# A hybrid delta-rule and attention layer on one core: the delta-rule query left unscaled, its squares joined to the output's norm, and new places for the steps of the mix stage

## What is computed

```python
def l2_normalize(x):
    return x * lax.rsqrt(jnp.sum(jnp.square(x), axis=-1, keepdims=True) + NORM_EPS)

q, k, v = jnp.split(silu(causal_depthwise_conv(qkv, conv_w)), ...)
q = l2_normalize(q); k = l2_normalize(k)
q = q * DK ** -0.5
...
o = einsum('bhck,bhkv->bhcv', q_dec, S) + einsum('bhcs,bhsv->bhcv', qk_intra, v_new)
S = S * g_last + einsum('bhck,bhcv->bhkv', k_dec, v_new)
...
o = rms_norm(o, norm_g) * silu(z)
```

## Time and profile before

| what | value |
|---|---|
| median of 3 runs (lowest to highest) | 2838.77 us (2835.92 to 2839.39) |
| the profiled execution, its own time | 2837.48 us |
| its span | 2835.7 us |
| PE busy, instructions | 2778.3 us (98%), 18295 |
| DVE busy | 2033.2 us (72%) |
| ACT busy | 1424.2 us (50%) |
| mix stage with its heads' ends | about 37 to 960 us |

### The profile page before, as it was taken

One profiled execution on the slowest core, in us unless ns is written; L12 is line 12 of the kernel. 1 busy time (PEld: TensorE's weight loads), 2 busy tenths in 40 slices (PEclk: granted clock), 3 DMA queues, 4 the chain that ended last, 5 costly groups with the idle time before them and its releaser, 6 DMA issues.

```text
span 2835.7 us, 51997 instructions
## 1 busy us (share of the span) xinstructions
PE 2778.3 (98%) x18295; PEld 2515.4 (89%) x18295; DVE 2033.2 (72%) x3714; ACT 1424.2 (50%) x2476; POOL 294.7 (10%) x261
## 2 busy tenths in 40 slices
PE   7999999999999999999999999999999999999998
PEld 7999999999999888888888888888888998888886
DVE  6777778777877656667775665656777677788876
ACT  5655665565556434444443443444545555455552
POOL 0000000000000000003630000000280001500024
PEclk9999999999999999999999999999999999999999
DMA  5444344434444455556555555555555444544444
GB/s 197 147 137 146 131 152 133 149 128 151 133 149 135 151 192 182 189 186 214 180 187 191 182 193 179 187 192 182 194 177 181 163 157 159 184 163 148 143 157 169
DMA packets 129664, 472.81 MB, mean 167 GB/s; under 512 B 15072, under 2 KB 15072, under 8 KB 129376
## 3 DMA queue, kind: packets, MB, share of 16 engines
q1 hardware_dynamic: 125568, 457.37, 49.1%
q0 software_dynamic: 3936, 13.34, 1.5%
HBM read 468.39 MB, written 2.25 MB: 166 GB/s over the span
## 4 chain that ended last, share of the span: by engine, by line
PE 88%; DVE 5%; issue 2%; ACT 2%; POOL 2%; DMA 1%; DVEq 0%; POOLq 0%; ACTq 0%
PE bank L305 35%; PE bank L306 18%; PE bank L307 9%; PE bank L308 8%; PE bank L309 8%; DVE mix_solve_m L1914 2%; PE bank L778 1%; DVE w_lo L281 1%; POOL late_sum L454 1%; POOL late_sq L450 1%; ACT w_hi L275 1%; PE bank L823 1%; PE bank L1034 1%; PE bank L1194 0%; ACT mix_f_p L1393 0%
## 5 line engine op out<-in xcount | busy, mean ns | idle before, releaser
L281 DVE TENSOR_TENSOR w_lo<-raw,w_hi 128x1024 fp32r<-128x1024 f32 x862 | 1058.7, 1253 | 160.5 <-ACT w_hi L275 158.0
L275 ACT ACTIVATE w_hi<-raw 128x1024 fp32r<-128x1024 f32 x862 | 897.0, 1054 | 452.5 <-PE bank L306 433.2
L305 PE MATMUL bank<-u,w_hi 128*128 128x512 f32 x2256 | 806.7, 399 | 0.0
L307 PE MATMUL bank<-u,w_hi 128*128 128x272 f32 (+2 forms) x2064 | 640.1, 310 | 9.1 <-DVE w_lo L281 7.5
L305 PE MATMUL bank<-ya,w_hi 128*128 128x512 f32 x1792 | 635.5, 399 | 2.8 <-DVE w_lo L281 2.8
L306 PE MATMUL bank<-u,w_lo 128*128 128x256 f32 x2256 | 634.8, 281 | 0.0
L309 PE MATMUL bank<-u,w_lo 128*128 128x272 f32 (+2 forms) x2064 | 590.0, 286 | 0.0
L308 PE MATMUL bank<-u,w_hi 128*128 128x272 f32 (+2 forms) x2064 | 589.7, 286 | 0.0
L305 PEld LDWEIGHTS bank<-u,w_hi 128*128 128x128 f32 x2256 | 424.3, 188 | 96.4 <-issue 2.8
L306 PE MATMUL bank<-ya,w_lo 128*128 128x256 f32 x1792 | 503.2, 281 | 0.0
L306 PEld LDWEIGHTS bank<-u,w_lo 128*128 128x128 f32 x2256 | 426.1, 189 | 0.5
(11 more groups left out here) (389 smaller groups left out, 3210.3 us busy)
## 6 DMA issues: line engine op xcount, KB each, us to landing
raw<-in_stream SPq DMA_DIRECT2D x864, 512.0 KB, 3.4
mix_row<-rows POOLq DMA_DIRECT2D x16, 408.0 KB, 4.4
xT<-in_xT SPq DMA_DIRECT2D x4, 544.0 KB, 5.5
mix_coef_m<-meta_rows POOLq DMA_DIRECT2D x16, 128.0 KB, 3.4
h<-in_xT POOLq DMA_DIRECT2D x1, 2048.0 KB, 10.0
out_dram<-h SPq DMA_DIRECT2D x4, 512.0 KB, 2.6
consts<-in_consts POOLq DMA_DIRECT2D x1, 1817.0 KB, 9.2
meta_rows<-mix_b_mat POOLq DMA_DIRECT2D x16, 1.0 KB, 2.5
```

Of the source, the lines that this page charges most:

```text
L275: act.activation(w_hi[:, slot], raw[:, slot], ACT.Copy).then_inc(hi_ready, 1)
L281: dve.tensor_tensor(w_lo[:, slot], raw[:, slot], w_hi[:, slot].bitcast(F32), ALU.subtract).then_inc(lo_ready, 1)
L305: pe.matmul(o, a, x, start=first, stop=False)
L307: pe.matmul(o, a, x[:, 0], start=first, stop=False)
```

## The change

- q of gdn is not normalised. The sum, root and scaling of gdn q are gone (one matmul on PE, two activations on ACT, one instruction on DVE per head), and `norm_of_head` counts four lengths.
- `q square` stays, with another scale, but writes into `fq` (free once the fox logits are done) and stands at 129. `o square` writes `sq` as before; a new DVE step, `o add` at 176, adds the two, and the o sum takes that. The o root uses a new constant column, `eps_o`.
- `qk` on PE and `q dec` on DVE wait for k's scaling or q's silu in place of q's scaling. The copy of the next head's fq waits for `o add`; the conv of the next q waits for `q square`.
- `meta` is in three parts of 2, 7 and 6 instructions.
- Many places in the three lists are new (below).
- In the later MLA stage two semaphores are merged into one, with the counts adjusted.

The diff, without the MLA stage's counts and the renamed arguments of `root`:

```diff
@@ constants
     add("eps", np.full((P, 1), EPS, np.float32))
+    add("eps_o", np.full((P, 1), EPS * P * 4 * EPS, np.float32))
@@ places of the mix steps
-            return n * 5 - 4 + ("gdn k", "gdn q", "fox q", "fox k", "gdn o").index(name)
+            return n * 4 - 3 + ("gdn k", "fox q", "fox k", "gdn o").index(name)
         PE_PLAN = (
-            (28, "columns"), (76, "k sum"), (81, "turn"), (87, "kk"), (94, "q sum"), (98, "transpose"), (100, "qk"),
-            (105, "prod", 1), (106, "fq sum"), (109, "step", 1), (110, "fk sum"), (111, "prod", 2), (118, "logits"),
-            (120, "step", 2), (120, "turn v"), (121, "prod", 3), (123, "step", 3), (123, "turn p"), (124, "prod", 4),
-            (126, "step", 4), (128, "fox out"), (128, "prod", 5), (132, "step", 5), (134, "meta v"), (135, "prod", 6),
-            (139, "meta state"), (141, "step", 6), (143, "k state", 0), (147, "v new", 0), (152, "state", 0),
-            (167, "k state", 1), (169, "v new", 1), (171, "state", 1), (179, "o sum"))
+            (28, "columns"), (76, "k sum"), (81, "turn"), (87, "kk"), (89, "qk"), (96, "fq sum"), (98, "transpose"),
+            (103, "prod", 1), (104, "fk sum"), (107, "step", 1), (110, "prod", 2), (113, "step", 2),
+            (115, "logits"), (116, "prod", 3), (119, "step", 3), (120, "turn v"), (124, "prod", 4), (124, "turn p"),
+            (125, "step", 4), (128, "prod", 5), (128, "fox out"), (131, "step", 5), (134, "prod", 6), (140, "meta v"), (142, "meta state"), (142, "step", 6), (143, "k state", 0), (148, "v new", 0), (152, "state", 0),
+            (167, "k state", 1), (169, "v new", 1), (171, "state", 1), (181, "o sum"))
         ACT_PLAN = (
-            (69, "k square"), (69, "k root"), (78, "cols"), (80, "decay"), (82, "q square"), (87, "turned"),
-            (93, "q root"), (101, "fq square"), (105, "fq root"), (105, "fk square"), (111, "fk root"), (114, "soft"),
-            (126, "f v"), (127, "f pt"), (127, "f out"), (137, "v new m"), (141, "state"), (152, "v new", 0),
-            (169, "v new", 1), (175, "o square"), (179, "o root"), (182, "y hi"))
+            (69, "k square"), (69, "k root"), (78, "cols"), (81, "decay"), (87, "turned"),
+            (90, "fq square"), (97, "fq root"), (98, "fk square"), (105, "fk root"), (114, "soft"),
+            (120, "f v"), (127, "f pt"), (127, "f out"), (129, "q square"), (138, "v new m"), (141, "state"),
+            (152, "v new", 0), (169, "v new", 1), (175, "o square"), (180, "o root"), (184, "y hi"))
         DVE_PLAN = (
-            (63, "silu", "k"), (70, "unit k"), (72, "g diff"), (72, "fox bias"), (78, "silu", "z"), (85, "decay b"),
-            (86, "b mat"), (90, "unit q"), (92, "qk"), (94, "q dec"), (96, "level", 0), (98, "mask", 1),
-            (110, "unit fq"), (111, "level", 1), (111, "unit fk"), (113, "mask", 2), (114, "logits"),
-            (114, "level", 2), (118, "mask", 3), (120, "soft"), (120, "level", 3), (120, "mask", 4),
-            (127, "level", 4), (127, "meta", 0), (127, "f out"), (127, "mask", 5), (128, "meta", 1), (128, "level", 5), (129, "final"), (135, "mask", 6),
-            (137, "level", 6), (146, "rhs", 0), (156, "state"), (167, "rhs", 1), (180, "y"), (182, "y lo"))
+            (63, "silu", "k"), (71, "unit k"), (72, "g diff"), (72, "fox bias"), (78, "silu", "z"), (85, "decay b"),
+            (86, "b mat"), (92, "qk"), (94, "q dec"), (96, "level", 0), (98, "unit fq"), (98, "mask", 1),
+            (105, "unit fk"), (106, "level", 1), (110, "mask", 2),
+            (112, "level", 2), (112, "mask", 3), (114, "logits"), (118, "level", 3), (120, "soft"), (120, "mask", 4),
+            (127, "level", 4), (127, "meta", 0), (127, "mask", 5), (127, "meta", 1), (127, "f out"), (128, "level", 5),
+            (128, "final"), (128, "meta", 2), (135, "mask", 6),
+            (137, "level", 6), (146, "rhs", 0), (156, "state"), (167, "rhs", 1), (176, "o add"), (182, "y"),
+            (184, "y lo"))
@@ PE
             def pe_qk(n):
-                pe.wait_ge(sem("unit q"), n)
+                pe.wait_ge(sem("unit k"), n)
+                pe.wait_ge(sem("silu"), 4 * n - 2)
@@ ScalarE
             def act_q_square(n):
                 act.wait_ge(sem("silu"), n * 4 - 2)
-                act.wait_ge(sem("length rs"), norm_of_head("gdn k", n))
-                square("gdn q", n, qT[:, META:], SEQ, 0.5)
+                act.wait_ge(sem("fox s"), n)
+                act.activation(fq[:], qT[:, META:], ACT.Square, scale=P * EPS ** 0.5).then_inc(sem("q squared"), 1)
             def act_o_square(n):
-                square("gdn o", n, bank[6][:, 0:SEQ], SEQ, 1.0)
+                act.activation(sq[:, :SEQ], bank[6][:, 0:SEQ], ACT.Square).then_inc(sem("o squared"), 1)
-                         "q root": lambda n: root("gdn q", n, SEQ, 1.0, ("unit k", n)),
-                         "o root": lambda n: root("gdn o", n, SEQ, 1.0 / P, ("unit fk", n)), "y hi": act_y_hi}
+                         "o root": lambda n: root("gdn o", n, SEQ, 1.0 / P, ("unit fk", n), "eps_o"), "y hi": act_y_hi}
@@ ScalarE, copies out of the projection banks
                             act.wait_ge(sem(evac_free[x][0]), evac_free[x][1] * head)
+                            if x == "fq":
+                                act.wait_ge(sem("length sq"), norm_of_head("gdn o", head))
@@ DVE
                     elif x == "q":
                         dve.wait_ge(sem("qk"), n - 1)
+                        dve.wait_ge(sem("q squared"), n - 1)
...
-                dve.wait_ge(sem("unit q"), n)
+                dve.wait_ge(sem("silu"), 4 * n - 2)
...
-                for j in (range(8), range(8, META - 1))[part_]:
+                for j in (range(2), range(2, 9), range(9, META - 1))[part_]:
...
+            def dve_o_add(n):
+                dve.wait_ge(sem("o squared"), n)
+                dve.wait_ge(sem("q squared"), n)
+                dve.tensor_tensor(sq[:, :SEQ], sq[:, :SEQ], fq[:], ALU.add).then_inc(sem("length sq"), 1)
...
-                         "unit q": lambda n: unit("gdn q", n, qT[:, META:], SEQ, 0.5 * HEAD_SCALE, "unit q"),
+                         "o add": dve_o_add,
```

More of the change, by code:

```diff
@@ L931, in _ @@
             steps_pe = {"k sum": lambda n: ones_sum("gdn k", n, TOK), "kk": pe_kk, "turn": pe_turn, "columns": pe_columns,
-                        "q sum": lambda n: ones_sum("gdn q", n, SEQ), "qk": pe_qk, "transpose": pe_transpose,
+                        "qk": pe_qk, "transpose": pe_transpose,
                         "fq sum": lambda n: ones_sum("fox q", n, SEQ), "fk sum": lambda n: ones_sum("fox k", n, TOK),
@@ L1021, in _ @@
                         if g and not k:
-                            pe.wait_ge(sem("c ln"), 1)
+                            pe.wait_ge(sem("c root"), 1)
                         pe.matmul(bank[2][:, :SEQ], const("ones"), norm_sq[:, k, :SEQ], start=k == 0,
@@ L1256, in square, with root @@
                 act.activation(sq[:, :width], src, ACT.Square, scale=pre).then_inc(sem("length sq"), 1)
-            def root(name, n, width, scale, last_unit):
+            def root(name, n, width, scale, last_unit, eps="eps"):
                 at_ = norm_of_head(name, n)
@@ L1262, in root @@
                 act.activation(ln_t[:, :width], bank[2][:, :width], ACT.Ln, scale=scale,
-                               bias=const("eps")).then_inc(sem("length ln"), 1)
+                               bias=const(eps)).then_inc(sem("length ln"), 1)
                 if last_unit[1]:
@@ L1300, in act_fq_square @@
                 act.wait_ge(tile_free[b], turn + 2)
-                act.wait_ge(sem("length rs"), norm_of_head("gdn q", n))
+                act.wait_ge(sem("length rs"), norm_of_head("gdn k", n))
                 square("fox q", n, fq[:], SEQ, 1.0)
@@ L1410, in _ @@
                          "q square": act_q_square,
-                         "q root": lambda n: root("gdn q", n, SEQ, 1.0, ("unit k", n)),
                          "turned": act_turned, "fq square": act_fq_square,
-                         "fq root": lambda n: root("fox q", n, SEQ, 1.0 / P, ("unit q", n)),
+                         "fq root": lambda n: root("fox q", n, SEQ, 1.0 / P, ("unit k", n)),
                          "fk square": act_fk_square,
@@ L1545, in c_root @@
                 act.activation(norm_ln[:, :SEQ], bank[2][:, :SEQ], ACT.Ln, scale=1.0 / MLA_RANK,
-                               bias=const("eps")).then_inc(sem("c ln"), 1)
-                act.wait_ge(sem("c ln"), g + 1)
+                               bias=const("eps")).then_inc(sem("c root"), 1)
+                act.wait_ge(sem("c root"), 2 * g + 1)
                 if g:
                     act.wait_ge(sem("c v"), RT)
-                act.activation(norm_rs[:, :SEQ], norm_ln[:, :SEQ], ACT.Exp, scale=-0.5).then_inc(sem("c rs"), 1)
+                act.activation(norm_rs[:, :SEQ], norm_ln[:, :SEQ], ACT.Exp, scale=-0.5).then_inc(sem("c root"), 1)
             def c_high(g):
@@ L2148, in c_scale @@
             def c_scale(g):
```

(2 more changed lines are left out.)

## The result

| | kernel before | changed kernel |
|---|---|---|
| median of the runs, us | 2837.79 (4 runs, 2835.92 to 2839.39) | 2812.97 (4 runs, 2811.71 to 2816.34) |
| profiled execution, span | 2835.7 | 2810.6 |
| forecast | | 2814.8 (2803 to 2832) |

The ratio is 0.9915, with a 95% interval of 0.9897 to 0.9932: faster by 24.8 us, where 24 were forecast. The changed kernel was run again later, beside other kernels (the last experiment): ratio 0.9922 (0.9909 to 0.9936). One of the 21 runs of the kernel before that stand beside e1, e2, e3 and e7 took 5672.67 us, twice the usual time, and is left out of their ratios.

A forecast was written before the change was run, and what follows sets the result against it. PE, busy for 98% of the span, was taken as the bound. Per head 0.44 + 2.0 - 0.6 - 0.3 = 1.5 us, 24 us over 16 heads, gave 2814.8 us; range 2803 to 2832, the forecast's own 2807 to 2826.

The forecast's parts named there:

- The q sum: One fp32 sum of 256 columns per head leaves PE: 0.44 us a head, 7.0 us over 16 heads.
- The addition's cover: DVE's addition of squares is ready before PE's o sum, moved two positions later, with 0.18 us to spare.
- Holes that go: PE's waits at step 5, the meta transpose, the fox transposes, products 3 and 6: 2.0 us a head to win from.
- Holes that come: New PE waits per head: 0.6 us at the probabilities' transposes, 0.04 at step 6, 0.24 at the second k-state product.
- The chain on DVE: From product 3's start on PE to the scaled probabilities: 4.94 us, against PE's arrival at the transposes after 4.33.
- The end of the half: Second k-state product, counted from step 4's start: PE there at 10.35 us, level 6 ready at 10.6.
- the sum came out at 1.5: Gain per head: 0.44 + 2.0 - 0.6 - 0.3 = 1.5 us, 24 us over 16 heads.
- A: Rival: only the q sum counts, the new order makes as much waiting as the old; 2831.8 us, chance 0.15.
- B: Rival: nearly all holes close, because DVE gets mask 3 sooner than worked out; 2802 us, chance 0.12.
- C: Rival: slower, transposes ahead of step 4 in PE's queue hold everything behind a late soft; 2851 us, chance 0.04.
- D: Rival: addition of squares late at the o sum, gain halves or vanishes; 2838 us within the noise, chance 0.04.
- The rule about the drain: DVE's next op waits for an empty pipe: 0.33 us a head longer to the transposes, 2820 us; forecast rejected it.

The follow-up runs named there:

- e1: The changed kernel's norm (q unscaled, squares added, no q sum) with all places of the kernel before; 2839.70 us, ratio 1.0010 to the kernel before.
- e2: As e1, with the o sum at 181 and the o root at 180; 2830.81 us, ratio 0.9979 to the kernel before.
- e3: The changed kernel with meta in parts of 8, 1 and 6 instead of 2, 7 and 6; 2816.16 us, ratio 0.9931 to the kernel before.
- e7: The changed kernel with the two qk matmuls at position 89 issued twice; 2821.30 us, ratio 0.9943 to the kernel before.
- e9: As e6, with rhs of the first chunk at 144, ahead of a low split; 2791.07 us, ratio 0.9839 to the kernel before.
- e5: The changed kernel with PE's step 4 and probability transposes both at 126, the step first; 2814.86 us, ratio 0.9924 to the kernel before.
- e10: The kernel before, q still normalised, with the changed kernel's places from position 112 on and meta in three parts; 2819.62 us, ratio 0.9943.
- e4: The changed kernel with DVE's mask 3 at 113, behind the low split of slab 112; 2800.62 us, ratio 0.9875 to the kernel before.
- e6: As e4, with mask 6 at 128 and level 6 at 136, each ahead of a low split; 2799.74 us, ratio 0.9871 to the kernel before.

## Why the prediction was right, and where it was off

- **The q sum.** Forecast 0.44 us a head. e7 puts four passes at 0.43, e2 the whole norm at 0.47. Right.
- **The addition's cover.** Forecast: the operand is ready 0.18 us before PE is there at the new place. In the changed kernel the addition runs from 448.32 to 448.74 and the o sum starts at 448.99, 0.11 after the stream matmul before it, so it waited for nothing. At the old place it would wait, and e1 shows that this would have eaten the gain of the sum.
- **Holes that go.** Forecast 2.0 us a head before. e9 has no hole, 53.71; the kernel before has 56.48, of which 0.47 are the norm: holes of 56.48 - 0.47 - 53.71 = 2.30 us. The term was 0.3 us short. By starts the places were right; left out were the late second passes, 0.10 each at product 3, step 5 and product 6 and 0.05 at the transposes (last section).
- **Holes that come.** Forecast 0.6 at the transposes, 0.04 at step 6 and 0.24 at L861, 0.9 in all. Measured 54.99 - 53.71 = 1.28: by starts 0.81, 0.03 and 0.20, and 0.24 more for late second passes (0.03, then 0.05 at product 6, 0.10 at step 6, 0.07 at L861). The chain on DVE was right: 4.13 us from product 3 to the reciprocal were forecast, 421.12 - 417.02 = 4.10 measured. The forecast left one part out of it: DVE's own level 3 stands between maxima and reciprocal and ends at 421.09, just when ScalarE's exps end too, so shorter exps alone would not have started the scaling sooner. PE came 0.1 us sooner (4.21 against 4.33), as I had priced the switches on top of passes, and the start after DVE's last scaling took 0.15 us where I had 0.05: these two make the 0.2 us that the hole at the transposes was short. The end of the half came out: counted from step 4's start at 422.99, PE could have started L861 at 10.40 and did at 10.60, against 10.35 and 10.6 forecast.
- **That the sum came out at 1.5 is in part luck.** Both sums of holes were low, by 0.3 and by 0.4 us. The unpriced second passes are in both (0.35 and 0.24), but the 0.2 at the transposes has causes of its own, and nothing made the two errors cancel as well as they did.
- **What the sum of holes leaves out.** I named the place where each hole lies and added them. e5 shows that one can't: the same 0.81 us came back elsewhere. What kept the forecast from this error is that it followed DVE's queue and PE's side by side to the end of the half. e3 (0.20 measured, 0.3 expected) and e5 (0.00, hardly any gain expected) came out by that reading.
- **The rivals.** A (only the norm counts) is refuted by e10 and e2; B (nearly all holes close) did not come with this change; it took the moves of e4, e6 and e9 on top; C and D did not come, D is what e1 shows at the old place.
- **The rule about the drain.** DVE instructions that don't depend on each other start before the one ahead has ended also in the changed kernel: silu k ends at 447.97 + 0.44 = 448.41, and the addition starts at 448.32. The Trainium skill, "VectorE: DVE Perf Modes", "The DRAIN you can't avoid", has the next op wait for an empty pipe, and adds in the same paragraph that a next op that is not held starts earlier. The prediction took the first half alone as the rule; by it the stretch of 4.10 us to the reciprocal would be at least 0.25 longer (three pairs of instructions at 0.08). The measurement shows the early starts, with which the added sentence agrees, so the forecast rightly went by the rows, and the page, read whole, does not speak against them.

Not tried: making ScalarE's high split behind the fox copies earlier, which e5's bracket names as the next link of the chain; e9 has no hole left for it to close.

## What to carry to other kernels

These rules come from this one kernel. Where one engine streams and others serve it in order, don't add up its waits: walk the serving queue and the streaming one side by side to the next point where they meet, because a wait removed on the streaming side comes back at the next meeting (e5), while the same wait removed on the serving side is time (e4). Look on the serving engine for work that needs nobody standing behind work that waits, here a weight split behind a mask: putting the split first was worth 0.85 us a head with one digit changed, against 1.49 for the whole change. And when work leaves the streaming engine, look whether its replacement is ready at the old place: e1 gained nothing until the reader stood two places later.

## What the runs showed of the hardware that was not expected

A late fp32 matmul often pays twice. An fp32 matmul of 128 columns goes as two passes, which start 0.11 us apart when it isn't late. When it waited, the second pass can be late as well: it starts 0.21 us after the first, and in the timeline the merged row is 0.49 us long in place of 0.39, as at L832 after the hole in the earlier trace rows, at L868 in e6, and at L779 in e1 (256 columns: 0.70 against 0.60). The size does not follow that of the hole: 0.10 us at step 6 of the changed kernel, which is late by only 0.03 (0.43 us long, in e3 0.33), 0.07 at L861, and at the transposes, behind the largest hole, only 0.02 to 0.03: their next pass starts 0.13 us after the first.

```profile
422.17 0.27 PE L901 MATMUL bank<-consts,mix_f_p 128*128 128x128 f32 x1
```

Adding these up gives the missing 0.3 us in the kernel before and 0.24 of the missing 0.4 in the changed one; e1 against e2 agrees, with 0.52 us of hole and 0.10 of second pass for a head distance 0.63 longer. Why the second pass is late, and why less at some places, was not tried.

A wait is shown later than its end: PE's mask waits start their matmul 0.06 us after DVE's end (437.21 + 0.28 to 437.55), and the transposes, which wait on two semaphores, 0.15 us after (421.32 + 0.57 to 422.04). Whether the second semaphore makes the difference was not tried.
